# Seven-product pairs in both halves of a feed-forward's down projection on Trainium2

## The reference

```python
x = x + 0.5 * swiglu(rmsnorm(x, ffn1_norm), w_gate1, w_up1, w_down1)    # block 1, d_ff 5632
h = rmsnorm(x, mix_norm)
x = x + concat(hgrn2(h @ w_in, ...), nsa(h @ w_in, ...)) @ w_out
x = x + mem_cross_attn(rmsnorm(x, xattn_norm), rmsnorm(mem, mem_norm), wq, wk, wv, wo)
x = x + 0.5 * swiglu(rmsnorm(x, ffn2_norm), w_gate2, w_up2, w_down2)    # block 2
out = rmsnorm(x, final_norm)
```

## Time and profile before

| what | value |
|---|---|
| median of 3 runs | 1977.46 us (1975.88 to 1978.14) |
| the profiled execution's own time | 1977.94 us |
| its span, first to last instruction | 1976.1 us |
| TensorE busy | 1956.9 us |
| VectorE busy | 1529.0 us |
| ScalarE busy | 1062.1 us |
| HBM read | 377.33 MB |

### The profile page before, as it was taken

One profiled execution on the slowest core, in us unless ns is written; L12 is line 12 of the kernel. 1 busy time (PEld: TensorE's weight loads), 2 busy tenths in 40 slices (PEclk: granted clock), 3 DMA queues, 4 the chain that ended last, 5 costly groups with the idle time before them and its releaser, 6 DMA issues.

```text
span 1976.1 us, 27433 instructions
## 1 busy us (share of the span) xinstructions
PE 1956.9 (99%) x10022; PEld 1616.1 (82%) x10022; DVE 1529.0 (77%) x1906; ACT 1062.1 (54%) x1305; POOL 13.6 (1%) x19
## 2 busy tenths in 40 slices
PE   9999999999999999999999999999999999999998
PEld 7888888888888888878777888888888888888886
DVE  7898899998886456766658675689999989888544
ACT  6555555555555444455555564555555555555443
POOL 0000000000000000000002000000000000000000
PEclk9999999999999999999999999999999999999999
DMA  9566666567766657565443465566666666666764
GB/s 300 184 202 199 202 193 209 183 201 235 228 222 193 194 165 220 176 198 157 137 124 114 163 202 169 160 227 207 193 191 209 187 200 205 203 208 202 247 192 147
DMA packets 148546, 382.69 MB, mean 194 GB/s; under 512 B 13424, under 2 KB 19824, under 8 KB 148080
## 3 DMA queue, kind: packets, MB, share of 16 engines
q1 hardware_dynamic: 146368, 378.70, 60.6%
q10 hardware_dynamic: 2096, 2.87, 0.4%
HBM read 377.33 MB, written 4.19 MB: 193 GB/s over the span
## 4 chain that ended last, share of the span: by engine, by line
PE 96%; ACT 1%; DMA 1%; DVE 1%; issue 0%; SPq 0%; DVEq 0%; ACTq 0%
PE psum L1889 54%; PE psum L1853 36%; PE psum L1876 2%; PE psum L2160 1%; PE psum L2203 1%; PE psum L1865 1%; DMA w_raw<-in_gu 0%; PE psum L2258 0%; ACT prob L886 0%; DMA w_raw<-in_w_in 0%; PE psum L2173 0%; DVE w_lo L1094 0%; ACT w_hi L584 0%; PE psum L2182 0%; ACT silu_gate L886 0%
## 5 line engine op out<-in xcount | busy, mean ns | idle before, releaser
L584 ACT ACTIVATE w_hi<-w_raw 128x1024 fp32r<-128x1024 f32 x694 | 725.7, 1056 | 674.3 <-PE psum L1853 324.7
L1094 DVE TENSOR_TENSOR w_lo<-w_raw,w_hi 128x1024 fp32r<-128x1024 f32 x694 | 835.7, 1221 | 310.1 <-ACT w_hi L584 307.9
L1889 PE MATMUL psum<-w_hi,xT_hi 128*128 128x512 f32 x920 | 360.2, 391 | 0.0
L1889 PE MATMUL psum<-w_hi,xT_lo 128*128 128x512 f32 x920 | 358.4, 390 | 0.0
L1889 PE MATMUL psum<-w_lo,xT_hi 128*128 128x512 f32 x920 | 358.3, 389 | 0.0
L1853 PE MATMUL psum<-w_hi,xT_hi 128*128 128x512 f32 (+1 forms) x544 | 213.0, 392 | 3.0 <-DVE w_lo L1211 2.8
L1853 PE MATMUL psum<-w_hi,xT_lo 128*128 128x512 f32 (+1 forms) x544 | 209.4, 385 | 0.0
L1853 PE MATMUL psum<-w_lo,xT_hi 128*128 128x512 f32 (+1 forms) x544 | 209.2, 385 | 0.0
L1889 PEld LDWEIGHTS psum<-w_hi,xT_lo 128*128 128x128 f32 x920 | 172.7, 188 | 36.1
L1889 PEld LDWEIGHTS psum<-w_lo,xT_hi 128*128 128x128 f32 x920 | 172.9, 188 | 35.1
L1889 PEld LDWEIGHTS psum<-w_hi,xT_hi 128*128 128x128 f32 x920 | 172.8, 188 | 35.1
(11 more groups left out here) (319 smaller groups left out, 2508.3 us busy)
## 6 DMA issues: line engine op xcount, KB each, us to landing
w_raw<-in_gu SPq DMA_DIRECT2D x351, 512.0 KB, 4.3
w_raw<-in_d SPq DMA_DIRECT2D x176, 512.0 KB, 4.6
w_raw<-in_w_in SPq DMA_DIRECT2D x88, 512.0 KB, 3.8
w_raw<-in_w_out SPq DMA_DIRECT2D x32, 512.0 KB, 3.8
w_raw<-in_cw SPq DMA_DIRECT2D x8, 512.0 KB, 4.0
w_raw<-in_wk SPq DMA_DIRECT2D x8, 512.0 KB, 4.5
w_raw<-in_wq SPq DMA_DIRECT2D x8, 512.0 KB, 3.7
w_raw<-in_wv SPq DMA_DIRECT2D x8, 512.0 KB, 3.6
```

The lines of the kernel that those rows point to most:

```text
L584: nc.scalar.activation(w_hi[:, slot], w_raw[:, slot], ACT.Copy).then_inc(w_hi_ready, 1)
L1094: nc.vector.tensor_tensor(w_lo[:, slot], w_raw[:, slot], w_hi[:, slot].bitcast(F32), ALU.subtract)\
L1889: mm = nc.tensor.matmul(psum[:, bank, :], act_t, w, start=(first and n == 0), stop=(last and n == 2))
```

## The change

- `DOWN_AT`, the places of pairs in the first half, goes from six to seven. The table is shared by both blocks.
- In block 1 the second half becomes one stage of 44 units too (`second` on each engine) with seven pairs at `SECOND_AT`, the first of them at its very first unit. It has weight-sum buffers of its own (index 1), which lie in the memory of the transposed tokens, and uses token-sum buffers 0 and 1.
- The preparation of its first pair is done by `ffn_down` in places 38 to 41. `out_halves` writes the result of a half and signals `first_out` after the first token tile; in the first half it now stands ahead of the last place's `step`. TensorE waits for `first_out` before the new pair's second unit.
- Memory squares, their variance and their loads move one or two places earlier. The transposes of x chunks 0 and 1 move to places 36 and 39, those of chunk 2 and the squares of chunks 2 and 3 into the input projection, whose first group goes to banks 6 and 7.

```diff
-DOWN_AT = (6, 12, 18, 24, 30, 36)
+DOWN_AT = (6, 12, 17, 22, 28, 33, 38)
+SECOND_AT = (0, 6, 12, 17, 22, 28, 33)
+SECOND_EV = SECOND_AT[-1]
+TURN_X, TAKE_X = (36, 39), (37, 40)
-MEM_SQ = (14, 15, 32, 33)
+MEM_SQ = (14, 15, 30, 31)
```

The new buffers:

```diff
+        t_f32 = [t_f32, nc.alloc_sbuf_tensor_at("t_f32_b", [P, 3, NW], F32, offset=at_T + 16384)]
+        t_lo = [t_lo, nc.alloc_sbuf_tensor_at("t_lo_b", [P, 3, NW], F32R, offset=at_T + 16384)]
+        t_hi = [t_hi, nc.alloc_sbuf_tensor_at("t_hi_b", [P, 3, NW], F32R, offset=at_T)]
```

SP's loads of the second half:

```diff
+                if u0 == U_DN1:
+                    for p in range(KF):
+                        u, kt = u0 + KF + p, SECOND_KT[p]
+                        if p in (8, 12):
+                            i = 2 + (p == 12)
+                            sp.wait_ge(unit_done, u0 + DOWN_EV + 2)
+                            sp.dma_start(x[:, :, i * NW:(i + 1) * NW], ...)
+                        load(u, u % SLOTS, w[P * kt:P * (kt + 1), 2 * NW:4 * NW].rearrange("p (g n) -> p g n", n=NW))
+                    return
```

On VectorE, the result of a half and the new second half:

```diff
+            def out_halves(c0):
+                for t in range(NT):
+                    last = nc.vector.scalar_tensor_tensor(
+                        out=x[:, t, c0:c0 + 2 * NW].rearrange("p (g n) -> p g n", n=NW), in0=psum[:, 2 * t:2 * t + 2, :],
+                        scalar=0.5, in1=comb[:, 2 * t:2 * t + 2, :], op0=ALU.mult, op1=ALU.add)
+                    if t == 0:
+                        last.then_inc(first_out, 1)
+                last.then_inc(x_ready, 2)
+
+            def second(u0, b_x, s_x, base_e):
+                for p in range(KF):
...
+                    if p == KF - 1:
+                        dve.wait_ge(unit_done, u0 + 2 * KF)
+                        dve.wait_ge(combined, base_e + 5)
+                        out_halves(2 * NW)
+                    if p + SLOTS < KF:
+                        second_ahead(u0 + KF + p, p + SLOTS)
+                    else:
+                        step(u0 + KF + p)
+                    if p + 6 in SECOND_AT:
...
+                        token_forms((i + 1) % 2, SECOND_KT[p + 6], ffT_hi, ffT_lo)
+                    if p + 4 in SECOND_AT:
...
+                        token_lo((i + 1) % 2, NP + ND + i + 1)
...
+                    if p == 16:
+                        lower_bound_args()
+                    if p == 24:
+                        lower_bound()
+                        trig_angles()
```

On VectorE, in `ffn_down`'s first half:

```diff
+                    if p == KF - 1:
+                        dve.wait_ge(unit_done, u0 + KF)
+                        dve.wait_ge(combined, base_e + 5)
+                        out_halves(0)
                     down_ahead(u0, p)
...
+                        if p == KF - 6:
+                            token_forms(1, 0, ffT_hi, ffT_lo)
+                        if p == KF - 4:
+                            token_lo(1, NP + ND + 1)
```

On TensorE, the new second half:

```diff
+            def second(u0, b_x, xr):
+                for p in range(KF):
+                    u = u0 + KF + p
+                    if p in SECOND_AT:
+                        i = SECOND_AT.index(p)
+                        pair_units(u, u % SLOTS, (i + 1) % 2, SECOND_KT[p:p + 2], hidden, NP + ND + i + 1,
+                                   NP * (FF_CHUNKS - 1) + ND + i + 1, i == 0, i == N2 - 1,
+                                   ((first_out, 1), (x_ready, xr + 2)) if i == 0 else None, 1)
+                    elif p - 1 not in SECOND_AT:
+                        both_unit(u, u % SLOTS, SECOND_KT[p], hidden, (3,) if p == 2 else (), p == KF - 1)
+                    if p in TURN_X:
+                        i = TURN_X.index(p)
+                        pe.wait_ge(p1_copied, P1_FFN)
+                        pe.wait_ge(combined, 3 * FF_CHUNKS + 2 + 1)
+                        batch(b_x + i, 0, x_tiles(i))
```

More of the change, by code:

```diff
@@ L78 @@
 DOWN_EV = DOWN_AT[-1]
-T_FFN, S_FFN = NP * (FF_CHUNKS - 1) + ND, NP + ND
-EV_FFN = 3 * FF_CHUNKS + 2
+SECOND_AT = (0, 6, 12, 17, 22, 28, 33)
+N2 = len(SECOND_AT)
+SECOND_KT = [0] * KF
+for _i, _p in enumerate(SECOND_AT):
+    SECOND_KT[_p], SECOND_KT[_p + 1] = 2 * _i, 2 * _i + 1
+_rest = [p for p in range(KF) if p not in SECOND_AT and p - 1 not in SECOND_AT]
+for _kt, _p in enumerate(_rest):
+    SECOND_KT[_p] = 2 * N2 + _kt
+SECOND_EV = SECOND_AT[-1]
+TURN_X, TAKE_X = (36, 39), (37, 40)
+T_FFN, S_FFN = NP * (FF_CHUNKS - 1) + ND + N2, NP + ND + N2
+EV_FFN = 3 * FF_CHUNKS + 2 + 5
+P1_FFN = FF_CHUNKS + 1
 FORMS_AT = ((3, 4, 11), (5, 7, 9))
@@ L793, in ffn_down @@
                             mem_squares(MEM_SQ.index(p))
-                        if p == 34:
+                        if p == 33:
                             root(N_MEM)
+                        if p == KF - 5:
+                            token_hi(1, NP + ND + 1)
+                if b_x is not None:
+                    second(u0, norm, b_x, s_x, xr)
+                    return
                 for n in (2, 3):
@@ L801, in ffn_down @@
                             squares(x, norm, k - 2)
[L802 to L812, removed]
-                                nc.scalar.activation(sin_t[:], ang[:, 1], ACT.Sin)
-                                nc.scalar.activation(cos_t[:], ang[:, 2], ACT.Sin).then_inc(trig_ready, 1)
                     if b_x is None and n == D_CHUNKS - 1:
@@ L831, in _ @@
             ffn_down(U_DN1, N_MIX, B_H1, B_MIXN, V_MIX, 0)
-            fill(4)
+            fill(1)
+            take(B_MIXN + 2, 0, xT_hi, 8, V_MIX + 8)
+            fill(2)
             take(B_MIXN + 3, 0, xT_hi, 12, V_MIX + 12)
+            fill(1)
+            act.wait_ge(x_ready, 4)
+            squares(x, N_MIX, 2)
+            fill(1)
+            squares(x, N_MIX, 3)
             root(N_MIX)
-            fill(4 * U_G - 4)
+            fill(4 * U_G - 5)
             act.wait_ge(z_ready, 4)
@@ L1410, in ffn_down @@
                     if b_x is not None:
+                        if p == 32:
+                            variance(N_MEM, 4, mem_sq)
                         if p == 34:
[L1412 to L1413 removed]
                             inverse(N_MEM)
[L1415 to L1421 removed]
+                        if p == KF - 6:
+                            token_forms(1, 0, ffT_hi, ffT_lo)
+                        if p == KF - 4:
+                            token_lo(1, NP + ND + 1)
+                if b_x is not None:
+                    second(u0, b_x, s_x, base_e + 5)
+                    return
                 for n in (2, 3):
@@ L1921, in last_units, with pair_units @@
                             mm.then_inc(c_first, 1)
-            def pair_units(u, slot, i, kts, src, s_count, n_pair, first, last, taken=None):
+            def pair_units(u, slot, i, kts, src, s_count, n_pair, first, last, taken=None, mem=0):
                 ka, kb = kts
@@ L1934, in made @@
                 def made(n):
-                    return t_hi[:, n, :], t_lo[:, n, :]
+                    return t_hi[mem][:, n, :], t_lo[mem][:, n, :]
                 pe.wait_ge(w_lo_ready, u + 1)
@@ L2002, in ffn_up @@
                 body(FF_CHUNKS - 1, True)
+            def second(u0, b_x, xr):
+                for p in range(KF):
+                    u = u0 + KF + p
[11 more added lines that the diff above has]
+                        batch(b_x + i, 0, x_tiles(i))
+                pe.wait_ge(combined, EV_FFN - 2)
             def ffn_down(u0, b_h, b_x, base_c, xr):
```

175 lines of the change are left out of this document (119 added, 56 removed).

## The result

| | before | after |
|---|---|---|
| median of 8 runs | 1976.87 us (1975.88 to 1978.14) | 1983.19 us (1978.94 to 1983.75) |
| the profiled execution | 1977.94 us, span 1976.1 | 1978.94 us, span 1977.1 |

The ratio is 1.0024, 95% interval 1.0014 to 1.0034; a second measurement gave 1981.72 us and 1.0025 (first experiment). The change makes the kernel some 5 us slower, a quarter of a per cent. I had forecast 1977.3 us and no change. One execution of after, at 4756.88 us, was disturbed: it is in the median (1982.95 us without it) but neither in the range nor in the ratio. The profiled execution of after is the fastest of its eight, and that of before stands 1.1 us above its median, so the two profiles differ by less than the medians.

A forecast was written before the change was run, and what follows sets the result against it. PE's own matmuls, 0.2267 us each, were taken to bound the changed stage. Terms -6.12 + 4.2 + 1.5 + 0.2 = -0.2 us gave 1977.3 us, no change; the stated range was 1973.6 to 1982.6 us.

The forecast's parts named there:

- What it removes: Both blocks' down projections: nine more pairs, three matmuls each, take 27 x 0.2267 = 6.12 us off PE's path.
- The turn: Between block 1's down-projection halves: PE waits for VectorE's first result operation, 4.2 us (3.5 to 4.7).
- The clock: Behind the stop between block 1's halves: PE's clock may halve to 1.2 GHz; chance 0.22, left out of the sum.
- rival 1: Clock falls while PE stands still between the halves: price 0 to 2.5 us, with 1.5 us 1978.8 us; chance 0.22.
- Loads: Block 1's down projection: loads landing late behind VectorE's bursts cost PE 0.2 us in all (0 to 1.3).
- VectorE's reserve of 0.35 us: Pairs five units apart: VectorE has 12.6 us of work in 12.92 us, so it fits with 0.35 us to spare.
- rival 2: Block 1's seven five-unit distances: late loads take VectorE's reserve, giving 1983.4 us (1981 to 1986); chance 0.22.
- Memory's squares: First half of block 1's down projection: squares at 30 and 31 only shift ScalarE work and two loads, costing nothing.
- The block: Lower bound and angles in mid second half, ahead of t_lo at unit 28: PE waits 1.5 us (0.7 to 2.9).
- The sum: Whole kernel: -6.12 + 4.2 + 1.5 + 0.2 = -0.2 us, so 1977.3 us and no change.
- the signs that I had named for a wrong forecast: No PE wait over 2 us between the halves, or PE's waits in block 1's down stage adding to over 9 us.

The follow-up runs named there:

- first experiment: The changed kernel measured once more with no edit, against the kernel before: 1981.72 us, ratio 1.0025.
- again: The changed kernel measured and profiled a second time with no edit: 1981.72 us, ratio 1.0025; its profiled execution took 1980.91 us.
- angles early: Changed kernel with the second half's angles moved from place 24 to 10 and the lower bound from 24 to 26: 1980.62 us, ratio 1.0017.
- squares early: Changed kernel with memory's last two squares at 26 and 27 instead of 30 and 31, their loads four units earlier: 1984.36 us, ratio 1.0037.
- the zeros' profile: Changed kernel with 14 PE products with a tile of zeros added before PE waits for x between the halves: 1981.56 us, ratio 1.0027.
- pairs-alone kernel: Kernel before with only the first halves' seven pairs and memory's last squares at 30 and 31: 1979.43 us, ratio 1.0015.
- six-first kernel: Changed kernel with six pairs in the first halves, the last at 36; block 1's second half keeps seven: 1978.22 us, ratio 1.0004.
- turn only: Changed kernel with six pairs in the first halves, the last at 34, nothing else edited: 1974.74 us, ratio 0.9989.
- six and six: Changed kernel with six first-half pairs (last at 34), angles at 10, lower bound at 26, and six second-half pairs six units apart: 1973.12 us, ratio 0.9982.
- first half placed: Kernel before with seven first-half pairs, memory's squares at 30 and 31, variance at 32, root at 33, inverse at 34: 1976.38 us, ratio 0.9995.

## Why the prediction was wrong

**What it removes: right.** 27 matmuls, 0.67 us of them in block 2. The 0.7 us more behind the last matmul is a term that I did not have.

**The turn: right in place and cause, a little short in size.** Taken 4.2 us, measured 4.47 in all four profiles of kernels that keep both tables and add no zeros (after, again, angles early, squares early); within its 3.5 to 4.7.

**The clock: the step that failed first.** I gave it a chance of 0.22 and left it out of the sum. It fell at the turn in all four of those profiles and cost 1.41 to 2.54 us; rival 1 had taken 1.5. The stop was longer than any over which the trace showed the clock held, and I should have put it in. The row that spoke for a clock that holds, the start of the earlier trace rows, was also the luck of one execution: in four of the thirteen profiles the clock fell at that very place (last section).

**Loads: the second step that failed.** "0.2 us in all (0 to 1.3)" was 1.04 us in the first profile and 2.91 in the second (last pair and others together, with what memory's squares have in them). I had counted VectorE's reserve of 0.35 us as if it were lost once. But VectorE itself frees the slots: when it is late, its own next loads start late, and it waits for them at the next pair (541.03 to 561.03 in "the changed kernel again"). It is the mechanism of rival 2, with loads of 6.21 and 5.98 us, at about half its size: single pairs 1 to 1.5 us late, not every pair. That rival 2's 1983.4 us is so near the measured median is luck: it had 4.5 us for the loads, 2.9 for the block and nothing for the clock.

**Memory's squares: "nothing" was wrong.** They lie in the distance from 33 and made VectorE wait 1.09 us for w_hi. In the first profile, where no load was late ahead of it, that made the pair 0.43 us late. Taking the squares away helped by 0.4 us only, as the loads were late as well.

**The block: right in cause, smaller than taken.** 1.5 us forecast, 0.83 and 0.78 measured; only with the turn shortened did it grow to 2.74. The waits of this stage are not independent terms. VectorE sets the dates, and what PE gains at one it waits for at the next. This the sum did not know; by the zeros' profile it is why they gained nothing.

**The sum.** With the values of the second profile: -6.12 + 4.47 + 1.41 + 0.78 + 2.91 = +3.45 us, against -0.2; it is what block 1's stage and block 2 show there (+4.13 and -0.67). With the parts outside them (0.7 us less up to the stage, 0.5 less between the two, 0.75 more behind the last matmul) the profiled execution is 3.0 us longer than that of before. The median of that measurement is 4.8 us above before's, but before's profiled execution is itself 1.0 us above its median, so 0.8 us are left open. In the first measurement the median is 6.3 us above before's and the profile is of the fastest execution; 4 us are open there. A trace shows waits only for profiled executions, but every execution has its mean granted clock on record, to a thousandth. In the first measurement it is 0.998 in the three that took 1978.9 to 1980.4 us and 0.996 or 0.997 in the four that took 1982.9 to 1983.8. A thousandth less over 1977 us is 4 us more at the low clock and costs up to 2 us (an estimate), so a clock that stayed low longer, or fell at a further place, can be much of this. Late loads can be the cause of such a fall as well; no run separates the two. Neither of the signs that I had named for a wrong forecast came: PE did wait over 2 us at the turn, and its waits in the stage add up to 5.1 us, not 9. Both signs were read from the list of waits, which does not hold what a slow clock costs or what other executions lose.

## What to carry to other kernels

When a change trades TensorE's work for VectorE's, look for the places where VectorE's order holds a result back, and put the last heavy group far enough ahead: here moving it by two to four places, and giving up one pair of 0.68 us in each block, took 3.5 to 7 us off. A reserve of a third of a microsecond per period is soon gone if the same engine also frees the buffers for its own loads. And do not sum waits in a row on one late engine: test the one that is last.

## What the runs showed of the hardware

The length of a stop alone does not say whether the clock falls. In the pairs-alone kernel it fell after PE idled 1.97 us, at 581 us; in the six-first kernel it held through 2.47 us at 674:

```profile
581.00:584.00 3.00, 2.84 (x7) 2.27 (x8) 2.96 (x5) 1.15 (x2) 0.00 (x0) 0.54 0.18 60
```

```profile
672.00:677.00 5.00, 2.53 (x12) 2.06 (x12) 4.90 (x8) 2.55 (x5) 0.00 (x0) 1.00 0.09 13
```

At the turn, where PE idled 4.3 us, it fell in all four profiles of kernels that let it idle so long. The Trainium skill (TensorE: Matmul & The Clock Gate, "Why this matters for your kernels") warns of idle gaps of a few microseconds; the turn agrees, and the falls after 1.97 us and, below, 1.81 us are not of that length. Once low behind a gap in the stage, the clock slowed 6 to 8 matmuls in three profiles (after, again, pairs alone) and 12 in two others (angles early, squares early) of nearly the same program.

The start of the kernel shows the same with one program. All thirteen profiles have there the code of the earlier trace rows, and PE idles behind its twelfth matmul of 128x512. In nine the clock held, in before through 2.48 us. In four (six first, turn only, six and six, first half placed) it fell, in six and six after 1.81 us:

```profile
11.52 0.62 PE L1987 MATMUL psum<-w_hi,xT_hi 128*128 128x512 f32 x1 [1.81 <-DVE w_lo L1273]
12.00:13.00 1.00, 1.00 (x4) 0.81 (x3) 0.97 (x3) 1.00 (x3) 0.00 (x0) 0.50 1.04 394
```

From the first matmul behind this gap to block 1's down stage these four took 472.1 to 472.2 us and the other nine 471.1. So one fall of the clock there costs 1.1 us, and whether it comes is a part of the difference between executions of any of these kernels.
